# The steps of a head's recurrence moved to the places where the next head's preparation visits TensorE

## The chip, the cores and the metric

The kernel runs on one core of one Trainium2 chip. The time is the device time of one launch in microseconds. TensorE multiplies and transposes, VectorE, ScalarE and GpSimd do elementwise work, and SyncE (SP) starts the loads of the weights.

## What is computed

One layer of a hybrid decoder for two groups of requests: a prompt of 256 tokens and 8 sequences of 4 tokens that continue from a given state, 288 token columns in all. Two token mixers run side by side on one projection, a gated DeltaNet and an mLSTM with 8 heads each; then come gates, an output projection and a gated ConvFFN. The change is in the recurrence of the DeltaNet, which per head and chunk is

```python
def step(S, xs):
    qc, kc, uc, wc, qkc, Gc = xs
    v_new = uc - jnp.einsum('bhld,bhdv->bhlv', wc, S)
    o = (jnp.einsum('bhld,bhdv->bhlv', qc * jnp.exp(Gc)[..., None], S)
         + jnp.einsum('bhij,bhjv->bhiv', qkc, v_new))
    g_last = Gc[..., -1]
    S = (S * jnp.exp(g_last)[..., None, None]
         + jnp.einsum('bhld,bhlv->bhdv', kc * jnp.exp(g_last[..., None] - Gc)[..., None], v_new))
    return S, o
```

The output `o` is then normalized over its 128 channels and multiplied by a gate. The kernel splits the prompt into two chunks of 128; the 8 short sequences are a third part with a state of their own.

## The kernel before

**The slots.** The first stage multiplies the normalized input by `w_in`. A weight tile of 2048 x 128 is multiplied in four slots, and there are 384 slots. In a slot TensorE makes 12 matmuls of 288 columns, the "products" (L1631 to L1633: upper part of weight and input, and the two cross terms, for 4 blocks). ScalarE in slot s makes the upper part of the weights of a block three slots ahead (`split_hi`, L498), which waits until the products of slot s - 1 are done; VectorE makes the lower part (`split_lo`, L505) from it. The buffers hold four blocks. After every fourth slot ScalarE copies the finished tile out of PSUM (L811, L812 or L834).

**The lanes.** All other work of the mixers stands in lanes. A lane is a generator that is run on each engine alike and yields the slot, counted from its start, at which its next step is due:

```python
PREP_AT = [16 + 28 * h for h in range(8)]
SCAN_AT = [44 + 28 * h for h in range(8)]
```

`front` (L392) goes through the slots; on TensorE the lanes' steps that are due come ahead of the slot's products, on the other engines behind the slot's split. Every engine executes its instructions in that order, so a step that waits holds up what stands behind it. Where two lanes are due in a slot, the preparation comes ahead of the recurrence. A stretch of mixer work between two slots' products is called a visit here.

**Preparation of head h** (`prepare`) starts at slot 16 + 28h. ScalarE and VectorE make the convolution (L845, then three passes L1289 at slots 0, 1 and 2), GpSimd clamps it (L606, slot 3), ScalarE makes the sigmoid in three passes (L858, L861, L864 at slots 3, 4, 5), VectorE multiplies (`qkv`, L1296, slot 6), GpSimd squares (`sq`, L614, slot 7), TensorE sums the squares at slot 8 (`norm`, L1673), ScalarE makes the factors from it (L871, L873), VectorE scales k and q at slot 9 (L1314, L1315), and TensorE transposes them at slot 10. From slot 12 to 24 the triangular inverse is made in levels: TensorE has a visit in every slot (L1710, L1716 and L1717, at the end L1722 and L1728). TensorE's visits are thus at slots 1, 8 and 10 to 24.

**The recurrence of head h** (`scan`) starts at slot 44 + 28h, the very slot at which the preparation of head h + 1 starts. Its steps on TensorE have names in the program: T0 (L1739), u0 (L1744, L1745), k1 (L1748), T1 (L1751), ksS (L1756, eight matmuls of 4 columns for the short sequences), u1 (L1760 to L1762), trS (a transpose), TS (L1767), oS (L1770 and eight of 4 columns, L1773), nrm (L1777), Ss1 and Ss2 (L1782). ScalarE copies the results that the next step reads (`vn0` L904, `vn1` L907, `ks_s` L910, `vn_s` L913), VectorE makes S and the residuals (L1371, L1374, L1377, L1380), GpSimd the masked copy and the scaling of the states (L635, L640). ScalarE's queue also loads the sample state (L902), which waits for the store of the head before (L934, L935). Seven of the eight recurrences have the next head's preparation beside them; head 7's has none, and head 0's preparation has no recurrence beside it.

After the DeltaNet come the mLSTM heads with lanes of their own from slot 274 on, and then the later stages, which the change doesn't touch.

Of the kernel before, what the change touches and what calls it, by code (L numbers as in the profile page):

```python
# [62 lines left out]
def build(nc, a, o):  # L63
# [56 lines left out]
    with ctx:  # L120
# [167 lines left out]
        bo, bw, bu = pm[:, 3], ps[:, 2], ps[:, 3]  # L288
# [252 lines left out]
        def _(pool):  # L541
# [83 lines left out]
            def scan(h):  # L625
                ec = handed[h % 2][-1]
                yield 11
                pool.wait_ge(*scan_a.after("vn_s", h))
                if h:
                    pool.wait_ge(*scan_t.before(h))  # L630
                else:
                    for steps in (gate_d, gate_a, gate_t):
                        pool.wait_ge(*steps.before(1))
                    pool.wait_ge(stored, 32)
                pool.tensor_tensor(vnm[:], vn_s[:].unsqueeze(1).to_broadcast([TS, NB, P]),  # L635
                                   seq[:].unsqueeze(2).to_broadcast([TS, NB, P]), ALU.mult).then_inc(*scan_p.done("vnm"))
                yield 13
# [4 lines left out]
                yield 17  # L642
# [72 lines left out]
        def _(act):  # L715
# [183 lines left out]
            def scan(h):  # L899
                yield 0  # L900
                act.wait_ge(ss_out, 32 * h)
                act.dma_start(ss[:], a["state_gdn_S"][0][:, h].rearrange("b k v -> k b v")).then_inc(ss_in, 16)  # L902
                act.wait_ge(*scan_t.after("T0", h))
                nc.scalar.activation(vn[0][:], bw[:, 0:P], ACT.Copy).then_inc(*scan_a.done("vn0"))  # L904
                yield 5
                act.wait_ge(*scan_t.after("T1", h))
                nc.scalar.activation(vn[1][:], bw[:, 2 * P:3 * P], ACT.Copy).then_inc(*scan_a.done("vn1"))  # L907
                yield 6
                act.wait_ge(*scan_t.after("ksS", h))
                nc.scalar.activation(ks_s[:], bu[:, 2 * P:2 * P + TS], ACT.Copy).then_inc(*scan_a.done("ks_s"))  # L910
                yield 10
                act.wait_ge(*scan_t.after("TS", h))
                nc.scalar.activation(vn_s[:], bu[0:TS, 2 * P + TS:3 * P + TS], ACT.Copy).then_inc(*scan_a.done("vn_s"))  # L913
                yield 13
# [3 lines left out]
                yield 14  # L918
                act.wait_ge(*scan_t.after("nrm", h))
                nc.scalar.activation(rso[:], bw[:, 0:T], ACT.Ln, bias=eps[:], scale=1.0 / P).then_inc(*scan_a.done("rs1"))  # L920
                yield 15
                act.wait_ge(*scan_a.after("rs1", h))
                nc.scalar.activation(rso[:], rso[:], ACT.Exp, scale=-0.5).then_inc(*scan_a.done("rs2"))
                yield 18
# [206 lines left out]
        def _(dve):  # L1131
# [230 lines left out]
            def scan(h):  # L1362
# [5 lines left out]
                yield 1  # L1368
# [9 lines left out]
                yield 8  # L1378
# [7 lines left out]
                for k, bank, at in ((0, bu, 16), (1, bw, 18)):  # L1386
# [5 lines left out]
                yield 19  # L1392
# [124 lines left out]
            for c, n in enumerate(CHUNKS):  # L1517
# [74 lines left out]
                else:  # L1592
                    for i in range(4):
                        at = 4 * n * i
# [11 lines left out]
        def _(pe):  # L1606
# [125 lines left out]
            def scan(h):  # L1732
                qe, ke, pt, kg, bv, xx, ec = handed[h % 2]
                c0, c1 = slice(0, P), slice(P, TP)
                yield 0
# [4 lines left out]
                yield 1  # L1740
# [5 lines left out]
                yield 3  # L1746
# [5 lines left out]
                yield 6  # L1752
# [5 lines left out]
                yield 7  # L1758
# [4 lines left out]
                yield 8  # L1763
                turn(bw[0:TS, 3 * P:], ks_s[:], P).then_inc(*scan_t.done("trS"))
                yield 10
# [9 lines left out]
                yield 14  # L1775
                pe.wait_ge(*scan_a.after("sqo", h))
                mm(bw[:, 0:T], ones[:], sqo[:], start=True, stop=True).then_inc(*scan_t.done("nrm"))  # L1777
                yield 15
# [6 lines left out]
                yield 17  # L1785
# [211 lines left out]
```

## Time and profile before

| | us |
|---|---|
| median of 3 runs | 2111.11 (2108.19 to 2113.13) |
| the profiled execution | 2110.57, its span 2108.6 |
| TensorE busy | 2027.2 |
| VectorE, ScalarE, GpSimd busy | 1204.2, 954.8, 200.1 |
| one head from norm to norm where a recurrence is beside it (244.48 to 315.64) | 71.16 |

Busy time of TensorE is modelled, since matmuls overlap: a product of 288 columns has a duration of 0.30 us, and the next one starts 0.13 us later. Starts are therefore the measure here, and idle time is what a row gives in brackets. The granted clock is 1.00 at 2.4 GHz and 0.50 at 1.2 GHz.

### The profile page before, as it was taken

The numbers are of one execution on the slowest core, as the hardware profiler recorded it, in microseconds if no ns is written. First come the engines' busy times: TensorE is split into PE (matmuls) and PEld (weight loads), VectorE is DVE, ScalarE is ACT, GpSimd is POOL, SyncE is SP. The second block draws the span as 40 slices with busy tenths as digits, with TensorE's granted clock in tenths as the row PEclk, the third lists the DMA queues.
The fourth block names the chain that finished last, engine by engine and source line by source line (L and its number), as shares of the span: only waits on it lengthen the run. The fifth ranks groups of instructions, "written<-read, shape, count | busy, mean of one in ns | idle before, by whom it ended". The sixth has DMA issues, their size and how long they took to land.

```text
span 2108.6 us, 39619 instructions
## 1 busy us (share of the span) xinstructions
PE 2027.2 (96%) x14675; PEld 1942.1 (92%) x14675; DVE 1204.2 (57%) x2398; ACT 954.8 (45%) x1863; POOL 200.1 (9%) x273
## 2 busy tenths in 40 slices
PE   6799999999999999999999999999999999999997
PEld 4798889889889999999989999999999999999997
DVE  3755555665564454554665556665466665466653
ACT  4444443444443444434554444554445544444543
POOL 3102110210110001010002200000000000000032
PEclk9899999999999999999999999999999999999998
DMA  6453544444445565654556756665566655566551
GB/s 157 114 127 109 140 122 120 120 132 125 122 122 146 152 170 137 165 143 144 160 154 161 191 142 160 162 161 158 163 163 162 164 161 156 163 165 165 146 153 62
DMA packets 564751, 307.89 MB, mean 146 GB/s; under 512 B 6979, under 2 KB 559083, under 8 KB 564327
## 3 DMA queue, kind: packets, MB, share of 16 engines
q1 hardware_dynamic: 522899, 278.22, 49.1%
q10 hardware_dynamic: 41548, 27.88, 4.6%
q8 instruction: 73, 1.20, 0.2%
q0 software_dynamic: 192, 0.26, 0.2%
q14 instruction: 39, 0.32, 0.0%
HBM read 293.32 MB, written 13.02 MB: 145 GB/s over the span
## 4 chain that ended last, share of the span: by engine, by line
PE 85%; DVE 4%; ACT 4%; issue 3%; POOL 2%; DMA 1%; ACTq 0%; DVEq 0%; POOLq 0%; SPq 0%
PE products L1631 25%; PE products L1633 24%; PE products L1632 24%; PE mixer L1611 2%; ACT w_hi L498 1%; PE mixer L1710 1%; PE products L1611 1%; DVE w_lo L505 1%; POOL sig L606 1%; PE mixer L1716 1%; PE mixer L1717 1%; PE products L1782 1%; PE mixer L1773 1%; PE mixer L1828 1%; DVE conv_out L1289 1%
## 5 line engine op out<-in xcount | busy, mean ns | idle before, releaser
L505 DVE TENSOR_TENSOR w_lo<-w_raw,w_hi 128x512 fp32r<-128x512 f32 x1037 | 717.7, 704 | 795.0 <-ACT w_hi L498 792.8
L498 ACT ACTIVATE w_hi<-w_raw 128x512 fp32r<-128x512 f32 x1037 | 636.7, 628 | 755.0 <-PE products L1633 732.4
L1631 PE MATMUL products<-h_hi,w_hi 128*128 128x288 f32 x1536 | 486.2, 317 | 7.1 <-DVE w_lo L505 5.1
L1632 PE MATMUL products<-h_lo,w_hi 128*128 128x288 f32 x1536 | 464.1, 302 | 0.0
L1633 PE MATMUL products<-h_hi,w_lo 128*128 128x288 f32 x1536 | 463.6, 302 | 0.0
L1631 PE MATMUL products<-f_hi,w_hi 128*128 128x288 f32 x1408 | 418.6, 297 | 1.0 <-ACT r L1059 1.0
L1633 PE MATMUL products<-f_hi,w_lo 128*128 128x288 f32 x1408 | 417.3, 296 | 0.0
L1632 PE MATMUL products<-f_lo,w_hi 128*128 128x288 f32 x1408 | 413.9, 294 | 0.0
L1631 PEld LDWEIGHTS products<-h_hi,w_hi 128*128 128x128 f32 x1536 | 298.4, 194 | 32.8 <-issue 20.6
L1632 PEld LDWEIGHTS products<-h_lo,w_hi 128*128 128x128 f32 x1536 | 298.3, 194 | 0.6
L1633 PEld LDWEIGHTS products<-h_hi,w_lo 128*128 128x128 f32 x1536 | 297.0, 193 | 0.0
L1631 PEld LDWEIGHTS products<-f_hi,w_hi 128*128 128x128 f32 x1408 | 265.4, 188 | 2.5 <-issue 1.9
L1632 PEld LDWEIGHTS products<-f_lo,w_hi 128*128 128x128 f32 x1408 | 267.0, 190 | 0.0
L1633 PEld LDWEIGHTS products<-f_hi,w_lo 128*128 128x128 f32 x1408 | 265.2, 188 | 0.0
L1631 PE MATMUL products<-u_hi,w_hi 128*128 128x288 f32 x704 | 208.9, 297 | 0.0
L1632 PE MATMUL products<-u_lo,w_hi 128*128 128x288 f32 x704 | 208.5, 296 | 0.0
L1633 PE MATMUL products<-u_hi,w_lo 128*128 128x288 f32 x704 | 207.9, 295 | 0.0
L1631 PEld LDWEIGHTS products<-u_hi,w_hi 128*128 128x128 f32 x704 | 132.4, 188 | 0.3
L1633 PEld LDWEIGHTS products<-u_hi,w_lo 128*128 128x128 f32 x704 | 132.4, 188 | 0.0
L1632 PEld LDWEIGHTS products<-u_lo,w_hi 128*128 128x128 f32 x704 | 132.3, 188 | 0.0
L1631 PE MATMUL products<-mix_hi,w_hi 128*128 128x288 f32 x256 | 77.4, 302 | 3.6 <-DVE mix_lo L1483 3.6
L1632 PE MATMUL products<-mix_lo,w_hi 128*128 128x288 f32 x256 | 76.9, 300 | 0.0
(409 smaller groups left out, 2422.0 us busy)
## 6 DMA issues: line engine op xcount, KB each, us to landing
w_raw<-in_w_in SPq DMA_DIRECT2D x96, 1024.0 KB, 6.0
w_raw<-in_w_up SPq DMA_DIRECT2D x88, 1024.0 KB, 5.9
w_raw<-in_w_down SPq DMA_DIRECT2D x32, 1024.0 KB, 5.8
w_raw<-in_w_out SPq DMA_DIRECT2D x16, 1024.0 KB, 7.6
w_raw<-in_w_down SPq DMA_DIRECT2D x16, 768.0 KB, 4.9
w_raw<-in_w_branch_a SPq DMA_DIRECT2D x8, 1024.0 KB, 5.5
w_raw<-in_w_branch_b SPq DMA_DIRECT2D x8, 1024.0 KB, 5.4
S_sample<-in_state_gdn_S ACTq DMA_DIRECT2D x8, 512.0 KB, 4.3
```

The source lines that it names most:

```text
L498: nc.scalar.activation(ring_slot(whi, whi2, n, ring), raw[:, s % slots, 4 * j:4 * j + 4], ACT.Copy).then_inc(hi_ready, 1)
L505: nc.vector.tensor_tensor(ring_slot(wlo, wlo2, n, ring), raw[:, s % slots, 4 * j:4 * j + 4], ring_slot(whi, whi2, n, ring).bitcast(F32), A ...
L606: pool.tensor_scalar(sg[:, 0:3 * GV], cv[:], SIG_MIN, None, ALU.max).then_inc(*prep_p.done("clamp"))
L1289: d(f"cv{t}{j}", stt(c, gq[h % 2][:, t, j:j + GV], gcw[:, j, t * H + h:t * H + h + 1], c, ALU.mult, ALU.add))
L1611: return nc.tensor.transpose(out, in_, ident[0:n, 0:n])
L1631: mm(out, w_hi, x_hi, start=start, stop=False)
L1632: mm(out, w_hi, x_lo, start=False, stop=False)
L1633: return mm(out, w_lo, x_hi, start=False, stop=stop)
L1710: last = mm(pm[0:n, 2, cc], nt[0:n, cc], xx[0:n, 0, cc], start=True, stop=True)
L1716: mm(pm[0:n, 0, cc], xx[0:n, 1, cc], psb[0:n, cc], start=True, stop=True)
L1717: last = mm(pm[0:n, 1, cc], psb[0:n, cc], xx[0:n, 1, cc], start=True, stop=True)
L1773: last = mm(bo[:, cc], ss[:, b], qe[:, cc], start=False, stop=b == NB - 1)
```

## The change

The numbers after `yield` in the recurrence lane are replaced, on all engines; no instruction is added or removed. T0 goes from slot 0 to 1, u0 from 1 to 8, k1 from 3 to 10, T1 from 5 to 12, ksS from 6 to 12, u1 from 7 to 14, trS from 8 to 14, TS from 10 to 16, oS from 12 to 18, nrm from 14 to 20, Ss1 from 15 to 21, Ss2 from 17 to 23. The steps of the other engines follow, the last ones and the store of the states from slot 19 to 24. Cut to TensorE and some of the others:

```diff
             def scan(h):
                 ec = handed[h % 2][-1]
-                yield 11
+                yield 17
                 pool.wait_ge(*scan_a.after("vn_s", h))
...
                 act.dma_start(ss[:], a["state_gdn_S"][0][:, h].rearrange("b k v -> k b v")).then_inc(ss_in, 16)
+                yield 1
                 act.wait_ge(*scan_t.after("T0", h))
                 nc.scalar.activation(vn[0][:], bw[:, 0:P], ACT.Copy).then_inc(*scan_a.done("vn0"))
-                yield 5
+                yield 12
                 act.wait_ge(*scan_t.after("T1", h))
...
-                yield 19
+                yield 24
                 act.wait_ge(*scan_d.after("ss2", h))
...
-                yield 1
+                yield 8
                 dve.wait_ge(*scan_t.after("u0", h))
...
-                yield 16
+                yield 21
                 dve.wait_ge(*scan_a.after("rs2", h))
...
-                yield 0
+                yield 1
                 pe.wait_ge(*prep_d.after("xx6", h))
...
-                yield 1
+                yield 8
                 if h == 0:
                     pe.wait_ge(*gate_d.before(1))
                 pe.wait_ge(*scan_a.after("vn0", h))
...
-                yield 3
+                yield 10
                 pe.wait_ge(*scan_d.after("S0", h))
...
-                yield 5
+                yield 12
                 pe.wait_ge(*scan_d.after("R1", h))
...
-                yield 6
+                yield 12
                 pe.wait_ge(ss_in, 16 * (h + 1))
...
-                yield 7
+                yield 14
                 pe.wait_ge(*scan_a.after("ks_s", h))
...
-                yield 12
+                yield 18
                 pe.wait_ge(*scan_a.after("vn_s", h))
```

The order of instructions shows it at three places of recurrence 1 and preparation 2. The first is TensorE from slot 5 to slot 8 before. The rows of L1631 are the first of a slot's 12 products:

```order
L1751 MATMUL products<-resid,x_xt_138 128x128 [waits scan_dve]
L1631 MATMUL products<-h_hi,w_hi 128x288 [waits block_lo_ready]
...
L1756 MATMUL products<-ke_134,S_sample 128x4 [waits S_in]
L1756 MATMUL products<-ke_134,S_sample 128x4 x7
...
L1760 MATMUL mixer<-qe_133,S 128x128 [waits scan_act]
L1761 MATMUL mixer<-pt_135,v_new_147 128x128
L1762 MATMUL products<-v_new_147,kg_136 128x128
...
L1673 MATMUL mixer<-sq,ones 128x288 [waits prep_act,prep_pool]
L1673 MATMUL mixer<-sq,ones 128x288
L1611 MATMUL products<-ident,ks_sample 32x128
```

The same engine with the change, from slot 1 to slot 8 (the lines are one higher, 1674 for 1673):

```order
L1612 MATMUL mixer<-ident,gdn_last_cols 27x128 [waits prep_dve,prep_pool]
L1612 MATMUL mixer<-ident,gdn_last_cols 27x128 x2
L1740 MATMUL products<-bv_137,x_xt_138 128x128 [waits scan_act,scan_dve,prep_dve]
L1632 MATMUL products<-h_hi,w_hi 128x288 [waits block_lo_ready]
...
L1674 MATMUL mixer<-sq,ones 128x288 [waits prep_act,prep_pool]
L1674 MATMUL mixer<-sq,ones 128x288
L1745 MATMUL mixer<-pt_135,v_new_146 128x128 [waits scan_act]
L1746 MATMUL products<-v_new_146,kg_136 128x128
```

Between T0 at slot 1 and norm at slot 8 TensorE has nothing but the 84 products of slots 1 to 7 there; u0 stands behind norm. The second place is VectorE at slots 1 and 2, before and with the change (`conv_out` is a pass of the convolution, `S` the copy of the state):

```order
L1289 SCALAR_TENSOR_TENSOR conv_out<-gdn_qkv_114,gdn_conv_w_t,conv_out 128x312 [waits prep_dve] x3
L1371 COPY S<-products 128x128 [waits S_stored,scan_pe]
L505 TENSOR_TENSOR w_lo<-w_raw,w_hi 128x512 [waits block_hi_ready]
L1289 SCALAR_TENSOR_TENSOR conv_out<-gdn_qkv_114,gdn_conv_w_t,conv_out 128x312 [waits prep_dve] x3
L1291 TENSOR_SCALAR sig<-z_143 128x288 [waits bank_free]
```

```order
L505 TENSOR_TENSOR w_lo<-w_raw,w_hi 128x512 [waits block_hi_ready]
L1290 SCALAR_TENSOR_TENSOR conv_out<-gdn_qkv_114,gdn_conv_w_t,conv_out 128x312 [waits prep_dve] x3
L505 TENSOR_TENSOR w_lo<-w_raw,w_hi 128x512 [waits block_hi_ready]
L1290 SCALAR_TENSOR_TENSOR conv_out<-gdn_qkv_114,gdn_conv_w_t,conv_out 128x312 [waits prep_dve] x3
L1292 TENSOR_SCALAR sig<-z_143 128x288 [waits bank_free]
```

The copy of the state has gone from between the second and the third pass. The third place is TensorE at slot 12 with the change, where T1 and ksS stand behind the preparation's transposes:

```order
L1612 MATMUL mixer<-ident,x_xt_131 128x128 [waits prep_dve]
L1612 MATMUL mixer<-ident,x_xt_131 128x128
L1612 MATMUL mixer<-ident,x_xt_131 32x32
L1752 MATMUL products<-resid,x_xt_138 128x128 [waits scan_dve]
L1757 MATMUL products<-ke_134,S_sample 128x4 [waits S_in]
L1757 MATMUL products<-ke_134,S_sample 128x4 x7
```

Before, oS stood there (L1770 and L1773), which is at slot 18 with the change.

## Rows read from the trace of the kernel before

**Rows 1.** The page: TensorE's busy time, share of the span, instructions.

```profile
PE 2027.2 (96%) x14675; PEld 1942.1 (92%) x14675; DVE 1204.2 (57%) x2398; ACT 954.8 (45%) x1863; POOL 200.1 (9%) x273
```

**Rows 2.** TensorE's waits: line, for whom; us in total, times, longest.

```profile
PE mixer L1673 <- POOL sq L614: 9.7, 8, 3.8
PE mixer L1760 <- ACT ks_sample L910: 6.7, 7, 1.0
...
PE mixer L1744 <- ACT v_new L904: 3.2, 7, 0.5
```

**Rows 3.** Stretches A, B, C of a head: busy time by engine, granted clock, DMA.

```profile
224.68:244.48 19.80, 17.58 (x134) 16.76 (x132) 12.90 (x24) 11.40 (x22) 4.93 (x4) 1.00 0.50 136
244.48:249.67 5.19, 4.54 (x30) 4.00 (x30) 3.53 (x12) 3.33 (x7) 0.64 (x3) 1.00 0.52 126
249.67:295.84 46.17, 46.17 (x336) 42.20 (x337) 24.37 (x48) 17.22 (x42) 5.06 (x5) 1.00 0.46 123
```

**Rows 4.** TensorE's timeline there: start, duration, instruction, idle before and releaser.

```profile
227.55 0.49 PE L1744 MATMUL mixer<-pt,v_new 128*128 128x128 f32 x2 [0.43 <-ACT v_new L904]
...
231.16 0.30 PE L1633 MATMUL products<-h_hi,w_lo 128*128 128x288 f32 x1
231.29 0.38 PE L1748 MATMUL products<-S,ke 128*128 128x128 f32 x2
...
231.65 0.29 PE L1632 MATMUL products<-h_lo,w_hi 128*128 128x288 f32 x1
...
236.62 1.84 PE L1756 MATMUL products<-ke,S_sample 128*128 128x4 f32 x16
238.32 0.38 PE L1631 MATMUL products<-h_hi,w_hi 128*128 128x288 f32 x1
...
244.48 1.24 PE L1673 MATMUL mixer<-sq,ones 128*128 128x288 f32 x4 [0.85 <-POOL sq L614]
...
249.67 0.87 PE L1611 MATMUL mixer<-ident,qkv 128*128 128x128 f32 x6 [0.65 <-DVE qkv L1315]
```

**Rows 5.** The chain of waits in stretch A: start, duration, engine and tile.

```profile
231.31 1.38 DVE conv_out L1289 x3
...
232.86 2.56 POOL sig L606
...
239.08 1.23 ACT sig L864
...
242.91 1.53 POOL sq L614
```

**Rows 6.** Timeline of VectorE and ScalarE in stretch A.

```profile
230.02 0.28 DVE L1371 COPY S<-products 128x128 f32<-128x128 f32 x1
230.62 0.69 DVE L505 TENSOR_TENSOR w_lo<-w_raw,w_hi 128x512 fp32r<-128x512 f32 x1 [0.31 <-ACT w_hi L498]
...
240.19 0.26 ACT L907 ACTIVATE v_new<-products 128x128 f32<-128x128 f32 x1
```

**Rows 7.** TensorE's timeline in head 0's preparation, and the wait at 1094.87.

```profile
101.43 2.29 PE L1673 MATMUL mixer<-sq,ones 128*128 128x288 f32 x4 [3.81 <-POOL sq L614]
...
110.06 0.88 PE L1611 MATMUL mixer<-ident,qkv 128*128 128x128 f32 x6 [1.51 <-DVE qkv L1315]
...
1094.87 0.60 PE L1631 MATMUL products<-mix_hi,w_hi 128*128 128x288 f32 x1 [3.56 <-DVE mix_lo L1483]
```

**Rows 8.** Stretches at a low granted clock; columns as in rows 3.

```profile
93.60:97.00 3.40, 2.62 (x11) 2.62 (x12) 2.32 (x6) 3.40 (x6) 0.22 (x1) 0.50 0.43 96
...
103.80:107.20 3.40, 3.40 (x16) 3.40 (x16) 1.52 (x9) 1.88 (x3) 0.00 (x0) 0.50 0.84 222
...
1100.50:1103.90 3.40, 3.40 (x15) 3.01 (x15) 0.00 (x0) 0.82 (x2) 0.00 (x0) 0.50 0.31 89
...
185.60:189.00 3.40, 3.40 (x17) 3.17 (x17) 0.06 (x1) 0.63 (x1) 1.85 (x1) 0.53 1.00 279
```

**Rows 9.** The stores of `S_sample` (L935): us from issue to landing.

```profile
DMA to landing us min/median/max: 3.3/3.6/4.9
```

More of the change, by code:

```diff
@@ L636, in scan @@
                                    seq[:].unsqueeze(2).to_broadcast([TS, NB, P]), ALU.mult).then_inc(*scan_p.done("vnm"))
-                yield 13
+                yield 19
                 pool.wait_ge(*scan_t.after("oS", h))
@@ L641, in scan @@
                     .then_inc(*scan_p.done("sse"))
-                yield 17
+                yield 22
                 pool.wait_ge(*scan_d.after("go", h))
@@ L902, in scan @@
                 act.dma_start(ss[:], a["state_gdn_S"][0][:, h].rearrange("b k v -> k b v")).then_inc(ss_in, 16)
+                yield 1
                 act.wait_ge(*scan_t.after("T0", h))
                 nc.scalar.activation(vn[0][:], bw[:, 0:P], ACT.Copy).then_inc(*scan_a.done("vn0"))
-                yield 5
+                yield 12
                 act.wait_ge(*scan_t.after("T1", h))
                 nc.scalar.activation(vn[1][:], bw[:, 2 * P:3 * P], ACT.Copy).then_inc(*scan_a.done("vn1"))
-                yield 6
+                yield 12
                 act.wait_ge(*scan_t.after("ksS", h))
                 nc.scalar.activation(ks_s[:], bu[:, 2 * P:2 * P + TS], ACT.Copy).then_inc(*scan_a.done("ks_s"))
-                yield 10
+                yield 16
                 act.wait_ge(*scan_t.after("TS", h))
                 nc.scalar.activation(vn_s[:], bu[0:TS, 2 * P + TS:3 * P + TS], ACT.Copy).then_inc(*scan_a.done("vn_s"))
-                yield 13
+                yield 18
                 act.wait_ge(*scan_t.after("oS", h))
@@ L917, in scan @@
                 nc.scalar.activation(sqo[:], bo[:, 0:T], ACT.Square).then_inc(*scan_a.done("sqo"))
-                yield 14
+                yield 20
                 act.wait_ge(*scan_t.after("nrm", h))
                 nc.scalar.activation(rso[:], bw[:, 0:T], ACT.Ln, bias=eps[:], scale=1.0 / P).then_inc(*scan_a.done("rs1"))
-                yield 15
+                yield 21
                 act.wait_ge(*scan_a.after("rs1", h))
                 nc.scalar.activation(rso[:], rso[:], ACT.Exp, scale=-0.5).then_inc(*scan_a.done("rs2"))
-                yield 18
+                yield 23
                 act.wait_ge(*scan_p.after("goz", h))
@@ L1371, in scan @@
                 d("S0", tc(S[:], bu[:, 0:P]))
-                yield 3
+                yield 10
                 dve.wait_ge(*scan_t.after("k1", h))
                 d("R1", stt(rr[:], bw[:, P:2 * P], nbeta[:, 1, h:h + 1], bv[:, 1], ALU.mult, ALU.add))
-                yield 7
+                yield 14
                 dve.wait_ge(*scan_t.after("u1", h))
                 d("S1", stt(S[:], S[:], ec[:, 1:2], bu[:, P:2 * P], ALU.mult, ALU.add))
-                yield 8
+                yield 14
                 dve.wait_ge(*scan_t.after("trS", h))
                 d("rs", stt(r_s[:], bw[0:TS, 3 * P:], nbeta[0:TS, 2, h:h + 1], bv[0:TS, 2], ALU.mult, ALU.add))
-                yield 16
+                yield 21
                 dve.wait_ge(*scan_a.after("rs2", h))
@@ L1385, in scan @@
                 dve.wait_ge(*scan_p.after("sse", h))
-                for k, bank, at in ((0, bu, 16), (1, bw, 18)):
+                for k, bank, at in ((0, bu, 21), (1, bw, 23)):
                     if k:
@@ L1391, in scan @@
                     d(f"ss{k + 1}", tt(half, half, bank, ALU.add))
-                yield 19
+                yield 24
                 dve.wait_ge(*scan_a.after("hi", h))
@@ L1745, in scan @@
                 mm(bu[:, 0:P], kg[:, 0], vn[0][:], start=True, stop=True).then_inc(*scan_t.done("u0"))
-                yield 3
+                yield 10
                 pe.wait_ge(*scan_d.after("S0", h))
                 mm(bw[:, P:2 * P], ke[:, c1], S[:], start=True, stop=True).then_inc(*scan_t.done("k1"))
-                yield 5
+                yield 12
                 pe.wait_ge(*scan_d.after("R1", h))
                 mm(bw[:, 2 * P:3 * P], xx[:, 1, c1], rr[:], start=True, stop=True).then_inc(*scan_t.done("T1"))
-                yield 6
+                yield 12
                 pe.wait_ge(ss_in, 16 * (h + 1))
@@ L1757, in scan @@
                 last.then_inc(*scan_t.done("ksS"))
-                yield 7
+                yield 14
                 pe.wait_ge(*scan_a.after("ks_s", h))
@@ L1762, in scan @@
                 mm(bu[:, P:2 * P], kg[:, 1], vn[1][:], start=True, stop=True).then_inc(*scan_t.done("u1"))
-                yield 8
+                yield 14
                 turn(bw[0:TS, 3 * P:], ks_s[:], P).then_inc(*scan_t.done("trS"))
-                yield 10
+                yield 16
                 pe.wait_ge(*scan_d.after("rs", h))
                 mm(bu[0:TS, 2 * P + TS:3 * P + TS], xx[0:TS, 1, TP:T], r_s[:], start=True, stop=True).then_inc(*scan_t.done("TS"))
-                yield 12
+                yield 18
                 pe.wait_ge(*scan_a.after("vn_s", h))
@@ L1774, in scan @@
                 last.then_inc(*scan_t.done("oS"))
-                yield 14
+                yield 20
                 pe.wait_ge(*scan_a.after("sqo", h))
                 mm(bw[:, 0:T], ones[:], sqo[:], start=True, stop=True).then_inc(*scan_t.done("nrm"))
-                yield 15
+                yield 21
                 pe.wait_ge(*scan_p.after("vnm", h))
@@ L1784, in scan @@
                 sample_update(0, bu)
-                yield 17
+                yield 23
                 pe.wait_ge(*scan_a.after("rs1", h))
```

## The prediction

> **What bounds the kernel now.** I read the page first, then the waits of TensorE, then one head in time. The page has TensorE busy for 2027.2 us, 96% of the span [rows 1]. That looks like a kernel in which every matmul costs its own time wherever it stands. The waits say that one place is different [rows 2]: the two square-sum matmuls of a head's preparation (L1673, "norm") wait for GpSimd's `sq` 8 times, 9.7 us in all, once for 3.8 us. The long one is head 0's, so the other seven are (9.7 - 3.8) / 7 = 0.84 us each. The recurrence's own steps wait for ScalarE's `v_new` and `ks_sample`, 7 times each. All seven heads that have a recurrence beside the next head's preparation therefore look alike, and one of them can stand for all.
>
> For that head (recurrence 1, preparation 2) the windows cut the period of 71.16 us in three [rows 3]. In A, 19.80 us from its slot 0 to norm, TensorE is busy for 17.58 us: it idles 2.22 us, namely 0.43 before u0 and 0.85 before norm [rows 4], and one of the waits for `ks_sample`, 6.7 / 7 = 0.96 [rows 2]. In B, 5.19 us from norm to the transposes of q, k, v, it idles 0.65 us. In C, 46.17 us, it never idles.
>
> What ends last in A is not TensorE. The chain of waits [rows 5] runs on VectorE's third convolution pass (1.38), GpSimd's clamp (2.56), ScalarE's three passes of 1.2 us with weight splits between them (the last is shown), VectorE's qkv and GpSimd's sq (1.53), and norm starts as sq ends. So A is set by a chain on the other engines, C by the sum of TensorE's work. **What is taken from A is worth only what it shortens that chain; what is put into C is paid in full.**
>
> **What one matmul costs, and what joining visits saves.** The lone matmul at slot 3 (L1748, two array instructions in the trace) stands between L1633 at 231.16 and L1632 at 231.65 [rows 4]. Without it, two products at the spacing of 0.13 us would take 0.27, so a visit of one matmul costs 0.22 us. The eight matmuls of 4 columns (L1756) take from 236.62 to 238.32, with the 0.08 us by which the next spacing is longer 1.78 us, 0.22 each too, inside one visit. So the trace shows no price of a visit beside that of its matmuls, and I value the merging of visits as such at nothing.
>
> The Trainium skill, "TensorE: Matmul & The Clock Gate", section "Wait — 56ns, not 53.3ns?", puts the smallest distance of two matmuls near 25 ns whatever their columns. By that the 16 instructions of L1756 would move 0.4 us instead of 1.78, and the total below would be 10 us lower; the trace disagrees at 0.11 us per instruction, and I use the trace.
>
> **What leaves A.** The diff moves u0 (2 matmuls, 0.44), k1 (0.22), T1 (0.22), L1756 (1.78) and u1 (3 matmuls, 0.66) to slots 8, 10, 12, 12 and 14. That is 3.3 us of TensorE work out of A; T0 moves from slot 0 to 1 and stays in it. On the chain it takes away little. VectorE's copy of S at 230.02 and its wait for product 1 go: without them the split can stand where the copy now stands, near 230.1 instead of 230.62, so the third pass and the clamp start 0.5 us earlier [rows 5, 6]. ScalarE's `v_new` copy at 240.19 (L907) goes from between the last pass and the split that VectorE needs before qkv: by its row at most 0.26 us, I take 0.2 [rows 6]. The chain is **0.7 us shorter**, A is 19.1 us, norm comes at 243.8 on the old time scale.
>
> TensorE has then 8 slots of 12 products at 0.134 (12.85), three transposes (0.33, at half a matmul's price) and T0 (0.22), 13.4 us. It idles 19.1 - 13.4, some 5.5 us: near 0.9 before slot 7 (the clamp ends at 234.9, ScalarE's first pass takes 1.2 and the two splits of slot 7's weights 1.3, so 237.5, while slot 6 is done by 236.6), and **near 4.6 before norm**. The waits of 0.43 and 0.95 go, but they were not on the path: the idle time moves and grows.
>
> **What is added behind norm.** u0 takes the place of the ks_sample transpose at slot 8 (0.44 for 0.11). The end of that slot's products releases the split, then k and q, for which slot 10 waits (0.65, B), so this chain is 0.3 longer. Into C, where nothing idles, go k1 0.22, T1 0.22, L1756 1.78, u1 0.66 and the transpose 0.11, together 3.0 us. The later steps (oS, nrm, Ss1, Ss2) change slot within C at the same count. Work: 3.0 + 0.3 - 0.7 = **+2.6 us a head, +18.2 for seven.** Bounds: 1.9 if u0 hides in the wait of 0.65 and the chain gains 1.1 (the two copies in full besides), 3.3 if it gains nothing. Recurrence 7 has no partner and no wait; its steps only move: 0.
>
> **The clock.** Head 0 shows what such idling does. Around its wait of 3.81 us the granted clock stood at 0.50 (1.2 GHz of 2.4) from 93.6 to 107.2, up to 5.8 us past the start of its norm [rows 7, 8]. A wait of 3.56 us before 1094.87 was followed by half clock up to 1103.9 [rows 7, 8]. The waits of 0.85 were not: A, B and C of the head have 1.00 [rows 3]. A wait of 4.6 us lies beyond the longest, so I take a fall at each of the seven.
> At half clock norm takes 2.29 us instead of 1.24 and the products have double length. There norm to the transposes took 110.06 - 101.43 = 8.63 us against 5.19 [rows 3, 7], 3.4 more, and that is the upper end. For the lower end I let it stand for 3.4 us from norm on, as long as a short stretch at half does in this trace [rows 8]: what passes in it takes up to twice its time, a loss of at most 1.7, of which some lies in the wait of 0.65: 1.4. I take the middle, 2.4, since head 0's return at 5.8 lies between the two: **+16.8 us for seven.** This is the term with the widest bounds, 10 to 24.
>
> The Trainium skill, same page, section "HAM oscillation — how this bites in real kernels", says that a wait between bursts of matmuls takes the clock to half again at each burst. It speaks against this change and gives the sum of 2146; read without it, by the work alone, the sum is 2129. The trace agrees in head 0.
>
> **Queues that steps are moved past.** ScalarE stores S and S_sample at slot 24 instead of 19, and waits for that store before it loads the next S_sample at slot 0. Nine slots lie between now, four then; a slot is at least 12 products, 1.6 us, so 6.4 us are left, and the landing took at most 4.9 [rows 9]. No wait, with 1.5 us in hand. The load has until slot 12 instead of 6. Of VectorE, `go` comes to the slot in which ScalarE makes its input; it holds the split of a block that is needed three slots later, so it costs nothing. GpSimd's `vnm`, `sse`, `goz` go to slots at which it has no preparation work.
>
> **Sum**, on the profiled execution (2110.57 us with a span of 2108.6; the median of three is 0.5 above, which I leave out): 2110.6 + 18.2 + 16.8 = 2145.6, **2146 us**, 1.7% slower.
>
> **Rivals.**
> 1. *The forecast*: chain-bound A, work paid in C, the clock falls. 2134 to 2158. Chance 0.60.
> 2. *The clock holds*: the same without its term. For it: the idle time is split, and norm's matmuls come at once behind it. Against: head 0. 2110.6 + 18.2 = 2129. Chance 0.18.
> 3. *Faster: A was TensorE's after all.* VectorE and ScalarE queue behind TensorE's steps, so the chain shortens with them, and the waits go: 2.22 + 0.65 = 2.9 us a head, 20 in all, 2090. For it: two of the three waits of A name recurrence steps. It decides at a chain shorter by 3.3 us, where the work added in C is paid; I find only 0.7, as the passes on GpSimd and ScalarE wait for each other, not for TensorE. Chance 0.08, and 0.05 for a balance within 0.2%.
> 4. *More falls of the clock.* Visits with oS (L1773, 16 narrow instructions) can be followed by 3.4 us at half, as from 185.6 [rows 8], 1.5 us each. In the new order two visits a head end in such a run behind transposes or other matmuls, L1756 at slot 12 and oS at slot 18. With the clock term at its top this gives 2160 and more. Chance 0.09.
> That the change doesn't move what it says is excluded by the order of instructions.
>
> **Numbers.** The predicted time is rival 1's, 2146. The range from 2125 to 2160 takes in most of 1 and 2, with the bounds of work (13 to 23) and clock (10 to 24), and leaves out 3, the balance and 4's far end. A measurement of this kernel tells 0.2% (4.2 us) from no change. Faster 0.08, same 0.05, slower 0.87.
>
> **What the profile after would show.** Norm waits for sq some 4.6 us in each of eight heads (37 us in all instead of 9.7), and the waits for v_new and ks_sample are gone. A is 19.1 us, B about 8, C 49. A stretch at half clock follows each norm. The busy time of VectorE, ScalarE and GpSimd stays. I am wrong in the first place if the wait before norm stays under 3 us (then the chain did depend on TensorE), in the second if it is long and the clock stays at 1.00, in the third if C grows by less than 3 us.

## The result, and the profile after

The changed kernel takes 2153.91 us (median of 4 runs, 2151.16 to 2157.58), the kernel before beside it 2112.08 us: ratio 1.0202, 95% interval 1.0185 to 1.0220. It is slower by 41.8 us. Its profiled execution took 2157.58 us with a span of 2155.6, 47.0 above that of before. That one stands at the upper end of its runs, so a sum made from the trace is some 5 us too high for the medians: the other three took 3.4 to 6.4 us less, at a mean granted clock of 0.970 to 0.972 instead of 0.968. Every count of stretches at half clock below is that of one profiled execution.

The page's line of busy time, and TensorE's waits (line, for whom; us in total, times, longest):

```profile
PE 2047.6 (95%) x14675; PEld 1963.9 (91%) x14675; DVE 1207.8 (56%) x2398; ACT 956.4 (44%) x1863; POOL 203.0 (9%) x273
```

```profile
PE mixer L1674 <- POOL sq L614: 36.0, 8, 4.6
...
PE products L1632 <- DVE w_lo L505: 10.4, 12, 3.2
PE mixer L1711 <- DVE decay L1357: 6.1, 8, 0.8
```

The same 14675 matmuls keep TensorE busy 20.4 us longer [rows 1]: that is not work, it is the same work at a lower clock. The wait before norm has gone from 9.7 to 36.0 us, and those for `v_new` and `ks_sample` are gone [rows 2]. The second line had 5 waits and 6.0 us before; the seven that came are 0.4 to 0.6 us each, 1.3 in recurrence 1, and stand in A, where they cost nothing as long as norm waits for sq. The third line is new: the triangular inverse's visit waits for VectorE's `decay`.

The windows of the head cut as before (A slot 0 to norm, B norm to the transposes of q, k, v, C the rest), first for recurrence 1, then for recurrence 2:

```profile
233.10:252.47 19.37, 13.50 (x102) 13.00 (x100) 12.08 (x21) 11.33 (x20) 5.48 (x4) 0.93 0.60 161
252.47:259.99 7.52, 6.88 (x33) 6.07 (x33) 3.37 (x11) 3.14 (x6) 1.23 (x3) 0.72 0.53 139
259.99:311.50 51.51, 50.68 (x364) 46.88 (x365) 25.23 (x51) 17.73 (x44) 5.50 (x5) 0.97 0.37 98
311.50:330.52 19.02, 13.91 (x103) 13.41 (x102) 12.76 (x22) 11.23 (x20) 4.93 (x4) 0.94 0.57 151
330.52:338.23 7.71, 7.07 (x32) 6.26 (x32) 3.37 (x11) 3.14 (x6) 1.24 (x3) 0.70 0.50 139
```

Against [rows 3], A is 0.4 to 0.8 shorter though TensorE is busy about 4 us less in it, B is 2.3 to 2.5 longer (7.5 to 7.9 us over the seven heads), C 5.3 longer. What stands at the borders, on TensorE's timeline:

```profile
252.47 2.29 PE L1674 MATMUL mixer<-sq,ones 128*128 128x288 f32 x4 [4.58 <-POOL sq L614]
...
259.99 0.87 PE L1612 MATMUL mixer<-ident,qkv 128*128 128x128 f32 x6 [0.64 <-DVE qkv L1316]
...
285.52 1.95 PE L1774 MATMUL mixer<-qe,S_sample 128*128 128x4 f32 x16
...
288.14 0.44 PE L1632 MATMUL products<-h_hi,w_hi 128*128 128x288 f32 x1
288.38 0.44 PE L1633 MATMUL products<-h_lo,w_hi 128*128 128x288 f32 x1
```

Norm now takes 2.29 us instead of 1.24, and behind the narrow matmuls of oS the products stand 0.24 us apart where [rows 4] has 0.13. Both are stretches at half clock (the columns are those of rows 3; the last but two is the granted clock):

```profile
249.70:256.50 6.80, 4.03 (x13) 3.46 (x14) 4.69 (x11) 2.39 (x6) 2.81 (x4) 0.51 0.47 113
287.20:290.60 3.40, 3.40 (x17) 3.40 (x17) 0.00 (x0) 0.41 (x1) 1.90 (x1) 0.53 0.00 0
```

The first lasts 6.8 us and begins 2.6 us ahead of this norm, while TensorE idles. There are seven of the first kind, one around each norm of heads 1 to 7, and seven of the second, behind each of their oS. The kernel before had none at these norms and three behind oS (185.6 [rows 8], 329.1, and 680.7 in recurrence 7). A stretch behind oS holds 14 products, 0.24 us apart instead of 0.134: 1.5 us lost. The seven are no seven independent cases: the heads follow each other every 78.4 us and these stretches every 78.5, so each head repeats the one before it almost exactly.

The new wait, on GpSimd, VectorE and TensorE:

```profile
279.83 1.89 POOL L635 TENSOR_TENSOR v_new_by_seq<-v_new_s,seq_of 32x1024 f32<-32x1024 f32 x1 [26.13 <-ACT v_new_s L914]
280.19 1.81 DVE L1357 TENSOR_TENSOR decay<-beta_decay,mask_level 128x256 f32<-128x256 f32 x1
282.06 0.71 PE L1711 MATMUL mixer<-x_xt,decay 128*128 128x128 f32 x4 [0.83 <-DVE decay L1357]
...
286.33 0.42 DVE L1357 TENSOR_TENSOR nt<-beta_decay,mask_level 128x256 f32<-128x256 f32 x1
```

VectorE's multiplication for an inverse level takes 0.42 us, but 1.81 when it starts under GpSimd's `v_new_by_seq` (`vnm`), and it ends 0.28 us after GpSimd's. TensorE waits 0.83 us for it, in each of seven heads. In the trace of before GpSimd's row met another level step of VectorE, at a place where TensorE had products to do. The step takes 1.75 of the 1.96 us of this row, and 0.43 in head 0, where no recurrence runs beside it:

```profile
251.88 1.89 POOL L635 TENSOR_TENSOR v_new_by_seq<-v_new_s,seq_of 32x1024 f32<-32x1024 f32 x1 [6.76 <-ACT v_new_s L913]
...
252.30 1.96 DVE L1337 TENSOR_TENSOR nt<-beta_decay,mask_level 128x256 f32<-128x256 f32 x2
```

The Trainium skill, "SBUF — State Buffer", section "SBUF: two separate sides", says that VectorE with two inputs in SBUF and GpSimd share a pair of ports, which whoever starts first holds for its whole instruction. The rows agree: 1.81 us instead of 0.42, ending just after GpSimd's.

### The profile page after: what moved, and what is told of

It reads as the page before. It is cut to its first block, busy times and chain, and to the rows that moved or that the text cites. A ratio compares the mean times of both kernels' runs of the same rounds, so it can differ in the third digit from the quotient of the medians.

```text
span 2155.6 us, 39619 instructions
## 1 busy us (share of the span) xinstructions
PE 2047.6 (95%) x14675; PEld 1963.9 (91%) x14675; DVE 1207.8 (56%) x2398; ACT 956.4 (44%) x1863; POOL 203.0 (9%) x273
## 4 chain that ended last, share of the span: by engine, by line
PE 83%; DVE 6%; issue 4%; ACT 3%; POOL 2%; DMA 1%; ACTq 0%; DVEq 0%; POOLq 0%; SPq 0%
PE products L1632 24%; PE products L1634 23%; PE products L1633 23%; PE mixer L1612 2%; DVE conv_out L1290 1%; DVE w_lo L505 1%; ACT w_hi L498 1%; PE mixer L1711 1%; PE products L1612 1%; POOL sig L606 1%; PE mixer L1674 1%; PE mixer L1717 1%; PE mixer L1774 1%; PE mixer L1829 1%; PE products L1783 1%
## 5 line engine op out<-in xcount | busy, mean ns | idle before, releaser
L1633 PE MATMUL products<-h_lo,w_hi 128*128 128x288 f32 x1536 | 469.4, 306 | 0.0
L1634 PE MATMUL products<-h_hi,w_lo 128*128 128x288 f32 x1536 | 468.7, 305 | 0.0
L1632 PEld LDWEIGHTS products<-h_hi,w_hi 128*128 128x128 f32 x1536 | 304.0, 198 | 37.4 <-issue 19.2
L1633 PEld LDWEIGHTS products<-h_lo,w_hi 128*128 128x128 f32 x1536 | 303.9, 198 | 0.6
L1634 PEld LDWEIGHTS products<-h_hi,w_lo 128*128 128x128 f32 x1536 | 302.3, 197 | 0.0
```

Source lines behind the costliest of these rows:

```text
L1632: mm(out, w_hi, x_hi, start=start, stop=False)
L1633: mm(out, w_hi, x_lo, start=False, stop=False)
L1634: return mm(out, w_lo, x_hi, start=False, stop=stop)
```

## The experiments

In all of them the kernel before ran on the same chip. In per cent of before, 0.1 is 2.1 us; the changed kernel stands at +2.02%.

**Half of the move.** Two kernels take one part of the recurrence's moves each (both cut against the kernel before). In the first the steps of the prompt (u0, k1, T1, u1) go behind norm as in the change and T0 to slot 1, while those of the short sequences (ksS at slot 6, trS 8, TS 10, oS 12) stay:

```diff
-                yield 1
+                yield 8
                 if h == 0:
                     pe.wait_ge(*gate_d.before(1))
...
-        scan_t = Steps(sem("scan_pe"), "T0 u0 k1 T1 ksS u1 trS TS oS nrm Ss1 Ss2")
+        scan_t = Steps(sem("scan_pe"), "T0 ksS u0 trS k1 TS T1 oS u1 nrm Ss1 Ss2")
```

> Only the prompt's steps take the new slots (T0 1, u0 8, k1 10, T1 12, u1 14); the short sequences' steps ksS, trS, TS, oS keep 6, 8, 10, 12. 1.5 us of TensorE's work a head leaves the stretch before norm instead of 3.3. Theory (the stretch is set by the chain to sq, what is put behind norm is paid in full, long waits cost clock): the chain is 0.5 us shorter, the wait before norm about 3.3 us, work behind norm 1.5, so +1.0 us a head, 7 us; if the clock falls at 3.3 us as it did after 3.56 and 3.81, 16 more: about 2135 us, and 2119 if it holds. Rival (TensorE's total sets the pace, the loss is something in the short sequences' steps): the time of before, 2112.

It took 2134.57 us, ratio 1.0115 (1.0097 to 1.0132), the 2135 expected. Norm waits some 3.6 us and is at half clock again:

```profile
248.28 2.29 PE L1675 MATMUL mixer<-sq,ones 128*128 128x288 f32 x4 [3.61 <-POOL sq L614]
```

```profile
247.90:251.30 3.40, 3.02 (x10) 2.38 (x10) 2.01 (x6) 1.23 (x3) 1.62 (x4) 0.52 0.21 46
```

The time came out as expected, but not for the reasons given. The stretch around norm lasts 3.4 us here, not 6.8; B is 7.1 to 7.2 us, 1.6 more than at full clock, so the clock at norm costs 11 us and not 16. In its place there are stretches at half behind oS in all seven heads and in recurrence 7, eight where the kernel before has three, which adds 5 x 1.5 = 7.5 us that the expectation did not have. oS stands at slot 12 in both kernels. The agreement with 2135 is in part luck.

The second moves only the steps of the short sequences (ksS to 12, trS 14, TS 16, oS 18); T0, u0, k1, T1, u1 stay at slots 0, 1, 3, 5, 7:

```diff
-        scan_t = Steps(sem("scan_pe"), "T0 u0 k1 T1 ksS u1 trS TS oS nrm Ss1 Ss2")
+        scan_t = Steps(sem("scan_pe"), "T0 u0 k1 T1 u1 ksS trS TS oS nrm Ss1 Ss2")
...
-                yield 6
+                yield 12
                 pe.wait_ge(ss_in, 16 * (h + 1))
```

> The other half: ksS, trS, TS, oS and all later steps take the new slots (12, 14, 16, 18 to 23), T0, u0, k1, T1, u1 keep 0, 1, 3, 5, 7. Theory: the chain is as long as before (19.8 us), 1.8 us of work a head moves behind norm, and VectorE's level step under GpSimd's masked copy adds 0.8: 2.6 a head, 18 us, about 2130; the idle 4.1 us is split in a wait before u1 (2.2) and one before norm (1.5), so the clock before norm holds; with a fall 2146. Rival (the loss is in moving the prompt's chain): the time of before, 2112.

2134.15 us, ratio 1.0118 (1.0101 to 1.0135). TensorE idles 2.11 us for ScalarE's `v_new` and 1.44 before norm, together 3.55 where the first kernel has 3.61 in one piece, and this norm is at full clock. These two rows, and two of its waits over the whole trace:

```profile
546.64 0.49 PE L1756 MATMUL mixer<-qe,S 128*128 128x128 f32 x2 [2.11 <-ACT v_new L908]
...
550.62 1.24 PE L1675 MATMUL mixer<-sq,ones 128*128 128x288 f32 x4 [1.44 <-POOL sq L614]
```

```profile
PE mixer L1756 <- ACT v_new L908: 14.9, 7, 2.2
...
PE mixer L1712 <- DVE decay L1358: 6.1, 8, 0.8
```

Each half costs a good half of the loss. TensorE's wait for `decay` is with the steps of the short sequences, to which `vnm` belongs. In four of the seven heads no half clock touches norm; in the other three it comes between the two waits, as here:

```profile
245.30:248.70 3.40, 3.03 (x12) 2.59 (x12) 3.40 (x8) 0.90 (x3) 2.21 (x4) 0.52 0.40 110
```

There it costs next to nothing: the second wait shrinks, and from u1 to norm it is 3.97 us (244.10 to 248.07) against 3.98 in the head shown (546.64 to 550.62); B is 5.33 against 5.08. But there are seven stretches at half where TensorE never idles, three behind ksS and four behind oS; one head has both kinds and the first head none. I had expected 2130, and it came out 4 above; four falls more than in the kernel before are 6 us.

**Idle time filled.** The changed kernel with 32 matmuls of 288 columns ahead of norm in heads 1 to 7, whose result nothing reads:

```diff
                 yield 8
+                if h:
+                    for _ in range(32):
+                        mm(pm[:, 1, 0:T], h_hi[:, 0, 0:P], h_hi[:, 1], start=True, stop=True)
                 pe.wait_ge(*prep_p.after("sq", h))
```

> The changed kernel, and ahead of norm TensorE makes 32 matmuls of 288 columns that nobody reads (4.3 us at full clock) in heads 1 to 7, while it would wait for sq. They write a PSUM bank that norm overwrites. Theory (the wait itself is hidden in the chain, what it costs is the half clock behind it): the wait before norm falls to about 0.3 us, no half clock follows norm, norm to the transposes takes 5.5 us instead of 7.5 to 7.9: 2.2 us a head, 15 us less than the changed kernel, about 2138. Rival (the half clock costs nothing, since the chain behind norm hides it; the loss is work alone): same time as the changed kernel, 2154, or more by the matmuls where they don't fit.

2138.97 us, ratio 1.0134 (1.0116 to 1.0151), 14 us faster than the changed kernel with 224 more matmuls. The same borders of B, and its clock:

```profile
479.75 1.24 PE L1677 MATMUL mixer<-sq,ones 128*128 128x288 f32 x4 [0.35 <-POOL sq L614]
...
485.27 0.88 PE L1612 MATMUL mixer<-ident,qkv 128*128 128x128 f32 x6 [0.65 <-DVE qkv L1316]
```

```profile
479.00:486.00 7.00, 6.01 (x43) 5.30 (x42) 4.85 (x13) 3.23 (x6) 1.99 (x4) 1.00 0.55 149
```

B is 5.52 or 5.53 us in all seven heads instead of 7.52 to 7.91, so the fall at norm costs 2.0 to 2.4 us a head, 2.2 in the mean, and it is the idle time that brings it on: norm still starts when sq ends. What is left above before, 1.34%, isn't this clock. Nine other stretches at half stand in the heads, six behind oS and three behind ksS; the changed kernel had seven. Their number isn't fixed for a kernel either: two of its four executions took 2136.6 and 2136.8 us at a mean clock of 0.982, the profiled one 2143.9 at 0.978.

**GpSimd one slot later.** The changed kernel with ScalarE's copy `vn_s`, which releases `vnm`, at slot 17:

```diff
-                yield 16
+                yield 17
                 act.wait_ge(*scan_t.after("TS", h))
```

> The changed kernel with ScalarE's copy vn_s at slot 17 instead of 16, so that GpSimd's masked copy vnm (1.89 us) starts a slot later and no longer stands under VectorE's step of level 3, which took 1.81 us instead of 0.41 there. Theory: the wait of 0.8 us a head before TensorE's level 3 product is gone, 5.7 us less than the changed kernel, about 2148. Rival (the long VectorE step has another cause, as the order of its queue): no change, 2154.

2143.47 us, ratio 1.0163 (1.0146 to 1.0180). TensorE's wait for `decay` is gone from the list; the step and `vnm` no longer meet:

```profile
278.63 0.42 DVE L1357 TENSOR_TENSOR decay<-beta_decay,mask_level 128x256 f32<-128x256 f32 x1
...
280.89 1.98 POOL L635 TENSOR_TENSOR v_new_by_seq<-v_new_s,seq_of 32x1024 f32<-32x1024 f32 x1 [29.48 <-ACT v_new_s L914]
```

The idle time alone was 7 x 0.83 = 5.8 us; the kernel gained 0.39%, 8 us. With the wait, four of the seven falls behind oS had gone too. From the transposes to the next T0 it is 50.98 us here where there is no fall (258.45 to 309.43), and 52.08 in the next experiment, which has the wait and no fall (257.04 to 309.12): the wait costs 1.1 us a head, 7.6 in all. With four falls at 1.5 that would be 13.6; the profiled executions are 15 us apart, the medians 8 to 10, with an interval of some 5 us either way. Here the stretches around two heads' oS, the first with a fall, the second without:

```profile
208.20:211.60 3.40, 3.40 (x17) 3.40 (x16) 0.69 (x1) 1.02 (x2) 0.91 (x1) 0.52 0.00 0
285.00:292.00 7.00, 7.00 (x55) 6.78 (x53) 2.32 (x4) 3.02 (x8) 1.79 (x1) 1.00 0.12 21
```

**The narrow matmuls apart.** The changed kernel with oS's eight matmuls of 4 columns four and four over slots 18 and 19, and ScalarE's step that waits for oS at slot 19 with them:

```diff
                 for b in range(NB):
+                    if b == 4:
+                        yield 19
                     cc = slice(TP + b * L, TP + b * L + L)
```

> The changed kernel with the eight narrow matmuls of oS in two visits, four at slot 18 and four at 19. Theory (the clock falls a second time in each head because of this run of narrow matmuls behind the four of the inverse): the 3.4 us at half that follow oS in seven heads are gone, 1.5 us each, 10 us less than the changed kernel, about 2144. Rival (these falls come from where the head stands in time, not from the run of narrow matmuls): as many falls at another place, 2154.

2145.59 us, ratio 1.0163 (1.0144 to 1.0182). None of the seven falls behind oS is left, although the wait for `decay` is there as before. The stretch that holds both halves:

```profile
282.59 1.05 PE L1776 MATMUL mixer<-qe,S_sample 128*128 128x4 f32 x8
...
285.61 0.95 PE L1776 MATMUL mixer<-qe,S_sample 128*128 128x4 f32 x8
```

```profile
283.00:290.00 7.00, 7.00 (x56) 6.89 (x56) 2.48 (x5) 2.63 (x7) 1.90 (x1) 1.00 0.01 2
```

Seven falls at 1.5 would be 10.5 us; 0.39%, 8 us, was measured, within the interval.

**All three cures**, to see whether anything else is hidden in the loss:

> The changed kernel with the three cures at once: 32 unread matmuls of 288 columns ahead of norm in heads 1 to 7, v_new_s one slot later (slot 17), and the matmuls of 4 columns of oS split four and four over slots 18 and 19. If the loss consists of work paid behind norm (18.2 us) and of falls of the clock and the new wait, with no further cost, then only the work remains, less the three falls behind oS that the kernel before has itself (1.5 us each, 4.5): 2110 + 18.2 - 4.5 = 2124, up to 2128. If there is a cost that none of the three cures touches, it stays at 2135 or more. No stretch at half clock should stand within the seven heads.

2125.09 us, ratio 1.0076 (1.0061 to 1.0090): within the 2124 to 2128 expected of work alone. The norms of heads 1 and 7, and the clock at the one place where it still falls, behind ksS at slot 12 in four heads:

```profile
172.38 1.24 PE L1677 MATMUL mixer<-sq,ones 128*128 128x288 f32 x4 [0.34 <-POOL sq L614]
...
619.03 1.24 PE L1677 MATMUL mixer<-sq,ones 128*128 128x288 f32 x4 [0.34 <-POOL sq L614]
```

```profile
262.10:265.50 3.40, 3.40 (x17) 3.11 (x16) 0.69 (x1) 1.08 (x3) 0.00 (x0) 0.51 1.05 292
```

I had expected no fall within the heads; there were four. From norm to norm a head takes (619.03 - 172.38) / 6 = 74.44 us. In the kernel before:

```profile
171.78 1.24 PE L1673 MATMUL mixer<-sq,ones 128*128 128x288 f32 x4 [0.85 <-POOL sq L614]
...
602.60 1.24 PE L1673 MATMUL mixer<-sq,ones 128*128 128x288 f32 x4 [0.84 <-POOL sq L614]
```

(602.60 - 171.78) / 6 = 71.80, two falls of its own in it. Less 1.5 us for each fall, 1.0 and 0.5 a head, it is 73.4 against 71.3: the moved work costs **2.1 us a head**. Two heads without any fall say nearly the same, 73.41 us (545.62 to 619.03) against 71.16 (244.48 to 315.64 in the kernel before), 2.25; and the heads with a fall took 74.87 to 75.12, so a fall is 1.5 us here too.

**Visits apart or joined.** The prediction valued the merging of visits at nothing. Two kernels add to the kernel before three single matmuls of 128 columns a head, whose result nothing reads, one with each in a visit of its own (slots 25, 26, 27), one with all behind slot 24's visit:

```diff
+                yield 25
+                mm(pm[:, 2, 384:512], ident[:], ones[:], start=True, stop=True)
+                yield 26
+                mm(pm[:, 2, 384:512], ident[:], ones[:], start=True, stop=True)
+                yield 27
+                mm(pm[:, 2, 384:512], ident[:], ones[:], start=True, stop=True)
```

> The kernel before with three added single matmuls of 128 columns a head (nobody reads them), in visits of their own at slots 25, 26 and 27, where TensorE otherwise has only products. Read in the trace from slot 24 to T0. My theory (a visit costs no more than its matmuls): 0.22 us each, 0.66 a head, and the same as with the three joined. Rival (each separate visit costs 0.1 to 0.2 us on top, as the change supposes): 0.96 to 1.26 a head.

> The same three matmuls a head joined to the visit at slot 24. My theory: 0.66 us a head, the same as apart. Rival: 0.3 to 0.6 us a head less than apart.

2114.27 us apart and 2114.20 joined, one execution each. TensorE's timeline from slot 24's visit to the next T0, first apart, then joined:

```profile
435.61 0.44 PE L1728 MATMUL mixer<-x_xt,p_sb 64*64 64x64 f32 x4
...
437.68 0.38 PE L1732 MATMUL mixer<-ones,ident 128*128 128x128 f32 x2
...
443.16 0.38 PE L1745 MATMUL products<-bv,x_xt 128*128 128x128 f32 x2
```

```profile
435.64 0.44 PE L1728 MATMUL mixer<-x_xt,p_sb 64*64 64x64 f32 x4
436.01 0.49 PE L1731 MATMUL mixer<-ones,ident 128*128 128x128 f32 x2
...
443.19 0.38 PE L1742 MATMUL products<-bv,x_xt 128*128 128x128 f32 x2
```

7.55 us both times, against 6.92 in the kernel before (433.12 to 440.04): 0.21 us a matmul, and nothing for the visit. From norm to norm over six heads it is 72.35 and 72.34 us a head. These are visits in which nothing waits; that is the case tested.

**The other way round.** If what stands ahead of norm is free and what stands behind it is paid, work should go into A. The kernel before with ksS at slot 3, trS 5, TS 6, oS 7:

```diff
-        scan_t = Steps(sem("scan_pe"), "T0 u0 k1 T1 ksS u1 trS TS oS nrm Ss1 Ss2")
+        scan_t = Steps(sem("scan_pe"), "T0 u0 k1 ksS T1 trS TS u1 oS nrm Ss1 Ss2")
...
-                yield 12
+                yield 7
                 pe.wait_ge(*scan_a.after("vn_s", h))
```

> The kernel before with work brought into the stretch ahead of norm instead of out of it: ksS at 3, trS at 5, TS at 6 and oS at 7 instead of 6, 8, 10 and 12, 2.3 us a head of TensorE's work out of the part in which it never idles. ScalarE's copies ks_s and vn_s come to slots 2 and 5. Theory: what fills idle time is free, but vn_s stands in the chain (0.25) and oS waits for it and ends behind the old start of norm (0.4): 1.6 us a head gained, 11 us, about 2100. Rival (ScalarE's copies and the waits put into the chain cost as much as is taken from the full part, or the narrow matmuls just ahead of norm let the clock fall): 2112 or more.

2103.78 us, ratio 0.9982 (0.9971 to 0.9992), 4 us above what I expected. The wait for sq is left in head 0 alone:

```profile
PE mixer L1675 <- POOL sq L614: 4.4, 1, 4.4
```

But five of the seven heads have the fall behind oS; the kernel before had three in all. So once more with the narrow matmuls of oS split over slots 7 and 8:

```diff
+                    if b == 4:
+                        yield 8
                     cc = slice(TP + b * L, TP + b * L + L)
```

> The kernel before with four visits moved into the idle time ahead of norm (ksS to slot 3, its transpose to slot 5, TS to 6, oS to 7; 2104 against 2109 before), and with oS's matmuls of 4 columns split four and four over slots 7 and 8. In the unsplit kernel five of the seven heads had 3.4 us at half clock behind oS, 1.5 us each. If the run of 16 narrow instructions brings these on there as it did behind norm in the changed kernel, they go and the time is 2104 - 7.5 = 2097 (2095 to 2099). If they are brought on by the idle time of A, they stay and the time is 2104.

2101.88 us, ratio 0.9957 (0.9945 to 0.9969). The stretch behind oS without the split, then with it:

```profile
386.00:389.40 3.40, 3.40 (x13) 2.81 (x12) 2.23 (x4) 2.05 (x6) 3.40 (x4) 0.52 0.00 0
```

```profile
382.00:390.00 8.00, 7.31 (x51) 6.68 (x51) 7.96 (x12) 3.94 (x9) 5.92 (x6) 1.00 0.05 11
```

No half clock is left in the seven heads. The gain over the unsplit kernel is 0.25%, 5.3 us, of the 7.5 I had put down for five falls, which lies within the two intervals; the 2097 expected (2095 to 2099) was missed by 5 us. This is the fastest version of the study, 0.43% faster than the kernel before.

Of these 9 us some 4.5 are the three falls behind oS that the kernel before has and this one hasn't. A head without a fall takes 70.41 us (242.95 to 313.36) against 71.16, 0.75 less, where I had expected 1.6. The 2.3 us of work are out of C, A is as long as before within 0.1, but B (383.96 to 390.68) is 6.72 us instead of 5.19. The rows show why:

```profile
384.55 1.89 POOL L635 TENSOR_TENSOR v_new_by_seq<-v_new_s,seq_of 32x1024 f32<-32x1024 f32 x1
...
384.78 4.07 DVE L505 TENSOR_TENSOR w_lo<-w_raw,w_hi 128x512 fp32r<-128x512 f32 x1
...
386.40 1.89 POOL L640 TENSOR_TENSOR S_sample<-S_sample,eg_last 128x1024 f32<-128x1024 f32 x1
```

VectorE's weight split, 0.68 us elsewhere, takes 4.07: it starts under `vnm` and ends 0.56 us after the GpSimd multiplication that follows `vnm` without a pause. It does so in every one of the seven heads (3.9 to 4.1 us), and behind it stand the scaled k and q for which the transposes wait. The early oS had released GpSimd's second multiplication into this place. No run here takes it away, so that it is worth the whole 1.5 us of B is argued from these rows.

## Why the prediction was right, and where it was not

The direction, the two terms of the sum and the range held (2125 to 2160, measured 2153.9); the predicted time was 8 us low, because two further costs stood at nothing in it.

*What bounds A.* Right. With about 4 us of TensorE's busy time gone, A is 19.02 us in the second head shown (forecast 19.1), norm waits 4.58 us (4.6), all eight waits together 36.0 us (37). Rival 3, in which A was TensorE's, is out. One difference in it was wrong: 19.1 - 13.4 is 5.7, not 5.5; TensorE idles 5.1 us, 4.58 before norm and 0.52 before slot 7, for which 0.9 was forecast.

*Work paid behind norm.* Forecast 2.6 us a head with bounds of 1.9 and 3.3. The kernel with all three cures measures 2.1 to 2.25. The changed kernel's own period, (644.11 - 173.55) / 6 = 78.43 us, is 6.63 above before; less 2.2 for the clock at norm, 1.5 for that at oS and 1.1 for the wait, and with 0.5 put back for the falls that before has itself, it leaves 2.3. The forecast was 0.3 to 0.5 too high, within its bounds.

*The clock at norm.* Forecast 2.4 a head; 2.0 to 2.4 by B with and without the idle time, 2.2 in the mean. Falls in each of seven heads, as said, and rival 2 (the clock holds) is out. The idle time is what brings them on: filled, they are gone. 3.6 us of it in one piece still has one at norm, half as long and at 1.6 us; in two pieces of 2.11 and 1.44, rival 2's "the idle time is split", four heads of seven have none there.

*Merging visits.* Right: nothing, measured at 0.00 us for three visits.

*"GpSimd's vnm, sse, goz go to slots at which it has no preparation work."* This step failed. It asked only whether GpSimd is free there, not who runs beside it. `vnm` now starts just ahead of VectorE's level step, on which TensorE waits at once: 0.83 us of idle time a head, 1.1 in the length of C, some 7.6 in all, as a term of zero in the sum. The row that warned stood in the trace of before (1.75 us for a step of 0.43).

*More falls of the clock.* Rival 4, at 0.09, is in part what happened: oS at slot 18 is followed by half clock in all seven heads, at its price of 1.5 us; ksS at slot 12 is not, in this kernel. Together with the wait this is 2.6 a head, less 0.64 for before's own three falls (4.5 / 7), 2.0 in place of nothing: C grew by 5.3 instead of 3.0. With work and clock at their measured size, 2110.6 + 15.8 + 15.7 + 14 = 2156, against the profiled execution's 2157.58. The sum stayed near because work and clock at norm were put 3 to 4 us too high together, and two terms of 14 us were left out: that the time lies in the range is owed to the range's width. So the chance of rival 4 was too low. Its condition, a narrow run behind other short matmuls in one visit, stood in the new order at two places a head; but it isn't a sufficient one, as ksS shows.

*The store of S_sample.* "No wait, with 1.5 us in hand" held in six heads of seven. The stores landed in 3.7 to 8.3 us, 3.8 at the median, against [rows 9]:

```profile
DMA to landing us min/median/max: 3.7/3.8/8.3
```

The longest is that of recurrence 0, issued at 226.56, and beyond the 6.4 us that were left. ScalarE's load of the next sample state is held until it lands:

```profile
234.92 0.40 ACTq L902 DMA_DIRECT2D S_sample<-in_state_gdn_S  x1
```

It goes out 1.83 us behind the split of its slot (233.09), in the next head 0.60 (312.42 and 311.82). A is 19.37 us in this head and 19.02 in the other; that these 0.35 us are the held queue's is argued, not shown. No matmul waited for the state itself.

What stays open: why a run of narrow matmuls is followed by half clock in some heads and not in others. Behind oS in one run it was two heads of seven in the kernel before, seven in the changed one and with the prompt's steps alone, four with the short sequences' alone, six with the idle time filled, three without the wait, five with A filled; behind ksS none, three or four. Split, it was none of seven in each of three kernels, whose heads stand at different distances. So the splitting is shown as a cure, and the narrow run as needed for these falls; the wait of 0.83 ahead of it is not what decides, since the prompt's half has seven without it. That a kernel's executions differ in mean clock (0.978 to 0.982 for the filled one) says that the order of instructions alone doesn't decide either.

## What to carry to other kernels

Before moving work to where it is cheap to issue, ask which engine ends each stretch: in a stretch that another engine's chain bounds, TensorE's work costs nothing on TensorE and also keeps its clock; taken out, it is paid in full where TensorE is the bound, and the clock on top. A step's new slot is to be read against every engine's row at that time, not only its own queue: GpSimd under a VectorE step that feeds TensorE cost 1.1 us a head, and where work was brought into A instead, two GpSimd steps in a row held a VectorE step for 4.07 us and B took back most of the gain. And break a run of narrow matmuls into two visits, since a visit cost nothing here.

## What the hardware showed that I had not expected

- A VectorE multiplication of 128x256 with both inputs in SBUF took 0.42 us alone and 1.81 us under a GpSimd multiplication of 1.89 us that started 0.36 us before it. Two such GpSimd multiplications without a pause held a VectorE operation of 0.68 us for 4.07 us.
- Sixteen matmul instructions of 4 columns in one run (1.95 us, with TensorE never idle behind them) were followed by 3.4 us at half clock in two to seven heads of seven, by kernel; two runs of eight, 3.0 us from start to start, in none of 21 heads.
- 224 more matmuls made the kernel 14 us faster.
